# Conditioning spread through the projections, selections of 128 columns, and ring slots given by a table

## The reference, cut to what matters

```
m = silu(c) @ ada_w[l] + ada_b[l]              # (1, 6*1024)
sh1, sc1, g1, sh2, sc2, g2 = split(m, 6)
h  = rms_norm(x, norm1_g[l]) * (1 + sc1) + sh1
# layer 0: y = [multi-scale pooling | latent attention over context and tokens] @ mix_w_out
# layer 1: y = conformer convolution of h
x  = x + g1 * y
h2 = rms_norm(x, norm2_g[l]) * (1 + sc2) + sh2
aff = softmax(h2 @ router_w)                   # 16 experts
gate, idx = top_k(aff.T, 64)                   # each expert takes its 64 best tokens
x  = x + g2 * scatter(gate * ((silu(h2[idx] @ wg) * (h2[idx] @ wu)) @ wd))
```

## Time and profile before

| | |
|---|---|
| median of 3 runs | 1656.19 us |
| profiled execution, its own time | 1656.06 us |
| its span, first to last instruction | 1654.0 us |
| mean granted TensorE clock | 0.961 |
| PE busy | 1448.9 us (88%) |
| PEld busy | 617.8 us (37%) |
| DVE / ACT / POOL busy | 433.7 / 244.2 / 76.4 us |
| moved by DMA | 499.30 MB, 302 GB/s over the span |

### The profile page before, as it was taken

How to read it: one execution, slowest core, us unless ns; L and a number is a source line. 1 busy time by engine, 2 the same in 40 slices (tenths; PEclk the granted TensorE clock), 3 DMA queues, 4 the chain that set the end, 5 groups by cost and what they waited for, 6 DMA issues and landing times.

```text
span 1654.0 us, 15790 instructions
## 1 busy us (share of the span) xinstructions
PE 1448.9 (88%) x6157; PEld 617.8 (37%) x6157; DVE 433.7 (26%) x829; ACT 244.2 (15%) x495; POOL 76.4 (5%) x153
## 2 busy tenths in 40 slices
PE   4999999998799889879888999995799889879877
PEld 2654555554333223223323444453233223223322
DVE  1212545635012202202205132535112202202204
ACT  2223333212010100100002211131010100100001
POOL 1000000000000000000001200000000000000001
PEclk9998999998799999999999999997799999999999
DMA  9738545006999999999999301305599999999994
GB/s 329 281 121 318 185 158 184 1 26 242 406 421 421 422 421 421 422 422 422 421 422 389 129 1 55 149 26 241 230 420 420 421 421 421 421 423 422 421 421 178
DMA packets 93955, 499.30 MB, mean 302 GB/s; under 512 B 6936, under 2 KB 7983, under 8 KB 44366
## 3 DMA queue, kind: packets, MB, share of 16 engines
q1 hardware_dynamic: 90302, 485.43, 72.5%
q0 software_dynamic: 2304, 8.39, 1.3%
q10 hardware_dynamic: 1296, 4.72, 0.7%
HBM read 492.23 MB, written 6.29 MB: 301 GB/s over the span
## 4 chain that ended last, share of the span: by engine, by line
PE 57%; DMA 33%; DVE 4%; issue 1%; ACT 1%; POOL 0%; POOLq 0%; DVEq 0%; SPq 0%; ACTq 0%
PE PS L957 20%; DMA ring<-in_exp_wu_dram 19%; DMA ring<-in_exp_wg_dram 13%; PE PS L760 7%; PE PS L638 3%; PE PS L792 3%; PE PS L607 3%; PE PS L681 3%; PE PS L969 3%; PE PS L834 3%; PE PS L619 3%; PE PS L627 2%; PE PS L855 1%; PE PS L775 1%; PE PS L768 1%
## 5 line engine op out<-in xcount | busy, mean ns | idle before, releaser
L957 PE MATMUL PS<-ring,arena 128*64 128x512 f32 x3008 | 673.1, 600 | 100.9 <-DMA ring<-in_exp_wu_dram 63.0
L957 PEld LDWEIGHTS PS<-ring,arena 128*64 128x64 f32 x3008 | 213.5, 138 | 547.9 <-issue 372.6
L1537 DVE TENSOR_TENSOR arena<-arena,PS 128x512 f32<-128x512 f32 x32 | 20.6, 684 | 542.2 <-PE PS L957 542.2
L969 PE MATMUL PS<-arena 128*128 128x512 f32 x256 | 124.2, 618 | 5.4 <-DVE arena L1548 3.2
L760 PE MATMUL PS<-ring,hT 128*128 128x512 f32 x256 | 113.7, 600 | 0.0
L1530 DVE TENSOR_TENSOR x<-x,PS 128x512 f32<-128x512 f32 x128 | 86.8, 686 | 31.8 <-PE PS L969 31.8
L1218 ACT ACTIVATE arena<-PS 128x512 f32<-128x512 f32 x32 | 17.4, 594 | 422.2 <-PE PS L957 422.2
L607 PE MATMUL PS<-consts,arena 128*128 128x128 f32 (+5 forms) x393 | 58.2, 293 | 21.9 <-DMA arena<-in_kv_norm_g_dram 14.0
L1548 DVE SCALAR_TENSOR_TENSOR arena<-PS,arena,g_row 128x512 f32<-128x512 f32 x32 | 22.6, 747 | 204.5 <-PE PS L957 204.5
L969 PEld LDWEIGHTS PS<-arena 128*128 128x128 f32 x256 | 40.5, 188 | 89.0 <-DVE x L1530 62.9
L760 PEld LDWEIGHTS PS<-ring,hT 128*128 128x128 f32 x256 | 49.0, 193 | 62.0 <-issue 62.0
(11 more groups left out here) (152 smaller groups left out, 1006.5 us busy)
## 6 DMA issues: line engine op xcount, KB each, us to landing
ring<-in_exp_wg_dram SPq DMA_DIRECT2D x64, 2048.0 KB, 20.4
ring<-in_exp_wd_dram SPq DMA_DIRECT2D x64, 2048.0 KB, 26.1
ring<-in_exp_wu_dram SPq DMA_DIRECT2D x60, 2048.0 KB, 23.6
ring<-in_ada_w_dram SPq DMA_DIRECT2D x24, 2048.0 KB, 9.9
ring<-in_conv_w_pw_dram SPq DMA_DIRECT2D x6, 2048.0 KB, 21.4
ring<-in_mix_w_out_dram SPq DMA_DIRECT2D x2, 2048.0 KB, 9.5
xn_rows<-xn ACTq DMA_DIRECT2D x8, 512.0 KB, 2.6
arena<-in_exp_wu_dram SPq DMA_DIRECT2D x2, 2048.0 KB, 19.0
```

What stands on the lines that cost most here:

```text
L957: last = nc.tensor.matmul(PS[64 * e:64 * e + 64, bank + half, :], lhs[:, k, 64 * e:64 * e + 64], w[:, e, kk, half * N:(half + 1) * N], sta ...
L969: nc.tensor.matmul(PS[:, 6 + i % 2, :], hot[:, (i // 2) * 128:(i // 2 + 1) * 128], y_rows[:, (i % 2) * N:(i % 2 + 1) * N], start=True, sto ...
```

## The change

1. **Selections.** `ada_select` takes both halves of `ada_rows` as one operand of 128 columns: 8 matmuls of 128 stationary columns in place of 16 of 64, for all 12 sections.
2. **Opening.** x and the context are loaded in 4 and 2 pieces behind the first two `ada` blocks. The thirteen small transfers move from SP to ACT. Section 0 is computed first; x and the context are transposed and copied unmodulated, and after section 1 DVE and ACT modulate them in place (context first).
3. **Conditioning.** Sections 2 and 3 move from the end of the projections in among them; 10 and 11 move from behind the routing to before the pooling and behind the values.
4. **Ring.** `SLOT_OF` gives each granule's slot by hand, `BEFORE` the granule that was in it. The output projection's weights go to the input projection's slots, and the first two expert quarters are issued before the late conditioning's later blocks.

```
 def l0_items():
-    o = [("params", (), "V")] + conditioning(0) + conditioning(1)
+    o = conditioning(0) + [("params", (), "V")]
+    o += [("xT", (k,), "VS"[k % 2]) for k in range(K8)]
     o += [("cT", (k,), "VS"[k % 2]) for k in range(K8 // 2)]
-    o += [("xT", (k,), "VS"[k % 2]) for k in range(K8)]
+    o += conditioning(1)
     o += [("zlat", (4,), "V"), ("zlat", (5,), "V"), ("zlat", (0,), "V"), ("latT", (4,), "S"),
...
+    o += conditioning(2)
...
+    o += conditioning(3)
...
+    o += conditioning(EARLY + LATE)
...
     o += [("value", (k,), "VS"[k % 2]) for k in range(KT)]
-    for s in range(2, EARLY):
-        o += conditioning(s)
-    return o + [("row", (2, 0), "S"), ("row", (2, 1), "S")]
+    return o + conditioning(SECTIONS - 1) + [("row", (2, 0), "S"), ("row", (2, 1), "S")]
...
-    if kind == "mix":
-        for s in range(EARLY + LATE, SECTIONS):
-            o += conditioning(s)
     return o + [("slotT", (), "V")]
...
+SLOT_OF = [0, 1, 2, 3, 4, 5, 0] + [1, 2, 3, 1] + [2, 3, 1, 2] + [3, 0, 4, 5]
...
             def ada_select(bank):
-                for h in range(2):
-                    for k in range(K8):
-                        last = nc.tensor.matmul(PS[64 * h:64 * h + 64, bank, 2 * k:2 * k + 2],
-                                                ada_rows[:, h, k::K8], pick, start=True, stop=True)
+                rows = ada_rows[:, :, :].rearrange("p a b -> p (a b)")
+                for k in range(K8):
+                    last = nc.tensor.matmul(PS[:, bank, 2 * k:2 * k + 2], rows[:, k::K8], pick, start=True, stop=True)
                 return last
...
+            load_pair(0, 0, range(2))
             for b in range(2):
                 sp.wait_ge(late_filled, b + 1)
...
-            for b in range(2 * SECTIONS - 2, 2 * SECTIONS):
-                load_ada(b)
-            load_pair(0, 0)
+            load_pair(0, 0, range(2, 12))
...
-            act_e.wait_ge(x_arrived, 16)
+            for n in range(OPENING):
+                drain(n)
             for t in range(T):
+                act_e.wait_ge(x_arrived[t], 16)
                 square(t, x[:, t, :], xn[:, t, :])
...
+                    if s == 1:
+                        for i, ks in ((1, (0, 1, 4, 5)), (0, range(0, K8, 2))):
+                            for k in ks:
+                                part = (hT, hcT)[i][:, k, :]
+                                last = v.tensor_scalar(part, part, amp[:, 0, 0, i, k:k + 1], cols[:, 0, 0, i, k:k + 1],
+                                                       ALU.mult, ALU.add)
+                            last.then_inc(modulated_v, 1)
```

More of the change, by code:

```diff
@@ L219, in arrivals @@
 def arrivals(g):
-    return 16 * sum(LATE if ORDER[n][0] == "late" else 1 + (n in TWO_DMAS) for n in range(g % SLOTS, g + 1, SLOTS))
+    return 16 * sum(LATE if ORDER[n][0] == "late" else 1 + (n in TWO_DMAS)
+                    for n in range(g + 1) if SLOT_OF[n] == SLOT_OF[g])
 def last_use(g):
@@ L446, in slot @@
         def slot(g):
-            return ring[:, g % SLOTS, :]
+            return ring[:, SLOT_OF[g], :]
         @block.sync
@@ L518, in _ @@
                            pool_w[0, :, :, :].rearrange("g p n -> p g n"))])
-            for b in range(4, 2 * EARLY):
+            for b in [*range(4, 2 * EARLY), *range(2 * (EARLY + LATE), 2 * SECTIONS)]:
                 load_ada(b)
@@ L534, in load_quarter, with load_pair @@
                              src[j, :, :, 2 * D * (q % 4):2 * D * (q % 4 + 1)]).then_inc(arrived, 16)
-            def load_pair(l, j):
-                for q in range(12):
+            def load_pair(l, j, quarters=range(12)):
+                for q in quarters:
                     if isinstance(j, int) and j == 0 and q in SPARE:
@@ L673, in fill @@
                     t = args[0]
-                    drained_through(place(0, "xT", K8 - 1))
+                    for modulated in (modulated_v, modulated_s):
+                        pe.wait_ge(modulated, 2 if t < T else 1)
                     a, b = (0, POOL) if kind == "zpool" else (POOL, MIX_IN) if t < T else (POOL + QL, MIX_IN)
@@ L1062, in drain @@
                     return
+                if kind == "sel" and args[0] == 1:
+                    act_e.wait_ge(drained_v, drains("V", n))
+                    act_e.wait_ge(drained_s, drains("S", n))
+                    for k in (2, 3, 6, 7):
+                        last = sc.activation(hcT[:, k, :], hcT[:, k, :], ACT.Identity, bias=cols[:, 0, 0, 1, k:k + 1],
+                                             scale=amp[:, 0, 0, 1, k:k + 1])
+                    last.then_inc(modulated_s, 1)
+                    for k in range(1, K8, 2):
+                        last = sc.activation(hT[:, k, :], hT[:, k, :], ACT.Identity, bias=cols[:, 0, 0, 0, k:k + 1],
+                                             scale=amp[:, 0, 0, 0, k:k + 1])
+                    last.then_inc(modulated_s, 1)
+                    return
                 if engine != "S":
@@ L1454, in _ @@
                 normalise(NORM["ctx"] + t, ctx_x[:, t, :], ctx_x[:, t, :])
-            for n in range(len(L0)):
+            for n in range(OPENING, len(L0)):
                 drain(n)
```

119 lines of the change are left out of this document (63 added, 56 removed), and 3 rows, old and new, of the table o.

## The result

The changed kernel takes 1671.7 us (median of 4 runs, 1670.8 to 1673.4); the kernel before, run beside it, 1656.1 us (4 runs). The ratio is 1.0091, with a 95% interval of 1.0078 to 1.0103: 0.9% slower, where 1673 us was forecast (1673.2 by the sum). The profiled execution took 1670.79 us for itself, 14.73 more than before's, with a span of 1668.8.

A forecast was written before the change was run, and what follows sets the result against it. PE was taken to set the pace ahead of the experts, and arriving weights in them. Opening -0.4, conditionings +19.9, late selections +1.9, way to experts -6.0 and experts +1.7 gave +17.1 on 1656.06: 1673 us, range 1656 to 1681.

The forecast's parts named there:

- The selection: In each conditioning: reading the strided operand paces it, so 128 columns take 3.84 us, ends 1.75 and 4.1.
- the rival: In the selections: a load has a fixed price whatever its width, 1.75 to 1.9 us each; 1638 us, chance 0.15.
- Conditionings among the projections: Before attention: four in line at 8.3 us, plus 4.2 of low clock, in place of 17.5 us: +19.9 us.
- to attention 93 us today, 113 expected: Sign in the profile after: the stretch from the first projection to attention grows from 93 to 113 us.
- Late selections: Six selections on PE's path, each 0.32 us longer: +1.9 us.
- From the choice to the experts: Cast to the experts' first matmul: without conditionings there, layer 0 becomes like layer 1, gather 4.3 us: -6.0 us.
- Experts: First matmul to last `wu` wait in layer 0: quarters loaded early win nothing, the stretch becomes like layer 1's: +1.7 us.
- Opening: Ahead of the projections: they start at 48.1 instead of 49.88, less 1.4 for low clock: -0.4 us, ends -4 and +3.
- The ring: Weight slots: block waits costed at nothing; the rival has two blocks late, +5 to +10, 1680 us, chance 0.06.
- The sum: Whole kernel: -0.4 + 19.9 + 1.9 - 6.0 + 1.7 = +17.1 us, giving 1673.2 us.
- cheap surroundings: Rival: long selection, but opening gives 4 us, clock falls behind one projection selection, blocks' 0.77 shrinks; 1665 us, chance 0.17.
- free width: Rival: a load costs the same whatever its width, so selections halve and low-clock stretches vanish; 1638 us, chance 0.15.

The follow-up runs named there:

- e1: The kernel before with only the selection of 8 matmuls of 128 strided columns: 1658.5 us, ratio 1.0008.
- e3: The kernel before with selections of 128 columns that ACT's copy lays side by side: 1629.3 us, ratio 0.9831.
- e2: The kernel before with the selection's two loops exchanged, so its 64-column strided matmuls alternate between the array's halves: 1631.5 us, ratio 0.9843.
- e12: The whole changed kernel with selections of 64 adjacent columns, halves in turns, and late blocks in slots 3 and 4: 1624.9 us, ratio 0.9804.
- e10: The changed kernel with sections 10 and 11 back under the choice, late blocks in slots 2 and 3, selections of 64 adjacent columns in turns: 1618.3 us.
- e5: The changed kernel with sections 2, 3, 10 and 11 and the ring put back, leaving the opening and wide strided selection: 1656.6 us, ratio 0.9997.
- e11: The whole changed kernel with selections of 64 adjacent columns, halves in turns: 1631.4 us, ratio 0.9840.
- e8: The kernel before with the opening and selections of 64 adjacent columns, halves in turns: 1617.7 us, ratio 0.9765.
- e4: The changed kernel with selections of 64 strided columns, halves in turns: 1643.5 us, ratio 0.9912.

## Why the prediction was right

**What bounds the kernel.** It held. PE paces all ahead of the experts, and each microsecond added there was a microsecond of time.

**The selection.** 3.84 us were forecast on the ground that reading the strided operand paces it; 3.94 came in line and 3.70 in attention. e1 shows that the width is worth nothing, e3 that the stride is the reason. The transposes' 188 ns for 128 strided columns, the best point of the rival, say nothing of a product. The 0.3 us that the old form is shorter I explained with the halves' loads overlapping where they meet; e2 shows that overlap at full size, and it is worth 26 us. That loads overlap at all was in the earlier trace rows: a load of 217 ns in steps of 120; how far they do for different halves took e2 to show.

**Conditionings among the projections.** Forecast +19.9, and 1.4 for the clock behind the opening; measured +23.4. The work was right: four times 8.3, against 17.5. The clock was sized too small. Behind the three new selections 4.2 us were forecast. From the end of each selection to the same point of the work it is 7.8, 15.5 and 8.8 us, where before has 6.0, 12.9 and 6.7 for the same pieces: 1.8 + 2.6 + 2.1 = 6.5 us. The 1.4 us for each came from windows at 0.66; the 5 us behind the second of them, from 105.50, read 0.50. The first projections took 19.16 us (49.02 to 68.18) against 17.48 (49.88 to 67.36), 1.7 for the forecast 1.4. Behind the last selection, with the gate's rows, nothing changed (4.7 us against 4.9 to attention). The sign given as "to attention 93 us today, 113 expected" ran to the gate's rows and not to attention (49.88 to 142.53 is 92.7); measured to the same place it is 116.3 after.

**Late selections.** Forecast +1.9, measured -1.1 for the stretch. The six are longer by 0.22 each, 1.3 us in all; attention's first matmul took 1.96 us where it was 3.58, as the clock was up again there. The forecast had no term for that, and none for the clock behind the sixth, which fell after and not before. The two sizes that are known, +1.3 and -1.6, leave -0.8 us open. e1, without the moves, has +0.7.

**From the choice to the experts.** -6.0 forecast, -5.7 measured; the gather went from 9.23 to 4.47, near layer 1's 4.32. e12 against e10 repeats it, -5.3, with 4.51 against 9.80 for the gather.

**Experts.** +1.7 forecast, +1.0 measured, which says little: over all fourteen kernels the stretch lies between 434.2 and 435.7 us, and it is 435.7 in e5, which has 10 and 11 under the choice. The -2.3 us behind them lie in layer 1, in code that the change doesn't touch. Early expert weights bought nothing that shows in this stretch.

**Opening.** It started the projections 0.9 us earlier, not 1.8, within what one execution differs from the next. e5 against e1 gives it some 2 us with the wide selection, as far as their intervals can tell.

**The ring.** I costed its waits at nothing, which held for the changed kernel, but for another reason than the one I gave. I looked at the distance from the freed slot to the use and not at the queue: several transfers that SP holds back behind one wait are issued together, and the next block lands behind all of them. The changed kernel has some 8 us to spare there, by the estimate above; e11, which needs 9 us less for that stretch, has none and loses 7.

**The sum.** +17.1 against +14.7. The stretch to attention came out 2.1 us dearer than forecast and the opening 0.9; the stretch of the late selections came out 3.0 cheaper, layer 1 2.3 and the experts 0.7. The forecast was good by its large terms, and it was luck that the misses in the others had opposite signs: the -2.3 us of layer 1 lie in code that the change doesn't touch. The cheap surroundings did not come, and nothing of the free width.

## What to carry to other kernels

Before a load is made wider, divide the time of a row of loads by their count: where the step is longer than for adjacent columns and doesn't follow the clock, the way the operand lies decides, and the copy that writes it may lay it out for nothing, as here; small products for the two column halves of the array belong in turns. Work under a wait of another engine is nearly free where it stands and dear anywhere that PE is full: moving two conditionings out from under the choice bought 5 to 8 us on the way to the experts and cost 12 to 20 before attention. When slots are set by hand, count for each wait the bytes that stand behind it in the queue, not only the time from freed to used.

## What the runs showed of the hardware

- A load of 64 stationary columns at a stride of 8 float32 takes a step of 120 ns at a granted clock of 1.00, and a row of 32 takes the same 3.5 us at 0.99 and at 0.71; 128 such columns 231 to 246 ns (3.70 or 3.94 us for 16). 128 adjacent ones take 105 ns at the full clock. The Trainium skill ("TensorE: Matmul & The Clock Gate", LDWEIGHTS) has the time follow the columns alone. These runs agree with that for 128 adjacent columns; strided ones do take twice as long for twice the columns, but more than twice the time of adjacent ones.
- Loads for the lower and the upper 64 columns of the array run side by side when they alternate: 63 ns a load in place of 120 with the stride, 34 ns for 64 adjacent columns (e8), where half of e3's 105 ns for 128 is 52.
- The length of a selection goes with the clock behind it, but does not fix it. In the 5 us behind the late selections the granted clock read about 0.66 for 11 of 12 of the long ones (3.5 to 3.7 us, before and after) and 1.00 for 16 of 18 of the short ones (1.7 to 2.0 us, e2, e3 and e4); the two that lost it, e2's fourth and e4's second, read 0.66. Among the projections one of about 2.1 us cost the clock in e4 behind the second and the third (14.35 us for a piece of 12.46, and 0.61 in its window), not behind the first. One of 1.1 us did not cost it once among the projections or in attention: 1.00 behind every one in e10, e11 and e12, and the same piece takes 12.65 us in e10. Why a selection of 2 us keeps the clock in one place and not in the other stays open; no run set out to tell.
- The first gather of the experts (one indirect transfer of 128 rows of 4 KB) lasts 4.3 to 4.6 us with the DMA engines otherwise at rest, and 8.8 to 9.8 us while expert quarters arrive.
